# Eight-row pieces for two query weight chunks, and a cache copy cut into pieces of 15 rows down to 1

## The reference, cut to what matters

```python
# per layer
h = x + merge(A(xn), B(xn), C(xn)) @ w_out        # xn = rms(x)
# PEER, xb = rms(h): 256 prompt tokens and 32 sample tokens
q = (xb @ wq).reshape(blk, 8, 2, 128)             # 8 heads, two half queries
s1 = einsum('nhd,kd->nhk', q[:, :, 0], k1)
s2 = einsum('nhd,kd->nhk', q[:, :, 1], k2)
...                                               # top 16 of each, top 16 of the sums: e, g
hid = gelu(einsum('nd,nhkd->nhk', xb, eu[e]))
y = h + einsum('nhk,nhkd->nd', g * hid, ev[e])
# the sample group's caches move on by four rows
kvs2048[l] = concat([cache_a_kv_w2048[l], new rows])[-2048:]
```

## Time and profile before

| | us |
|---|---|
| median of 3 runs | 1813.08 |
| lowest and highest of them | 1811.39, 1815.6 |
| the profiled execution, its own time | 1812.33 |
| its span in the trace | 1810.3 |

### The profile page before, as it was taken

One profiled execution on the slowest core, in us unless ns is written; L12 is line 12 of the kernel. 1 busy time (PEld: TensorE's weight loads), 2 busy tenths in 40 slices (PEclk: granted clock), 3 DMA queues, 4 the chain that ended last, 5 costly groups with the idle time before them and its releaser, 6 DMA issues.

```text
span 1810.3 us, 18420 instructions
## 1 busy us (share of the span) xinstructions
PE 1546.9 (85%) x5782; PEld 826.0 (46%) x5782; DVE 1109.4 (61%) x2783; ACT 605.1 (33%) x1873; POOL 696.6 (38%) x682
## 2 busy tenths in 40 slices
PE   8999999998888787788789999989888877877777
PEld 5779644454333232233257885545443333322221
DVE  3545765676888774444535367475878878644444
ACT  2332432333334332222333344233333323322222
POOL 5211443455444443334313014435455444433341
PEclk9999999999889989999799999999999989899999
DMA  9899999999999999999979999999999999999996
GB/s 337 343 377 378 382 422 421 413 421 421 421 421 421 422 421 422 422 422 421 422 282 399 380 387 371 421 421 418 421 421 421 422 421 421 422 422 421 422 423 288
DMA packets 102839, 730.03 MB, mean 403 GB/s; under 512 B 14994, under 2 KB 16115, under 8 KB 21973
## 3 DMA queue, kind: packets, MB, share of 16 engines
q0 software_dynamic: 90432, 627.75, 84.2%
q1 hardware_dynamic: 11760, 100.48, 14.0%
q10 hardware_dynamic: 548, 0.62, 0.1%
HBM read 724.54 MB, written 48.10 MB: 427 GB/s over the span
## 4 chain that ended last, share of the span: by engine, by line
DMA 45%; PE 37%; DVE 11%; ACT 3%; issue 2%; DVEq 2%; ACTq 1%; POOL 0%; POOLq 0%
DMA arena<-peer_uv,idx 26%; PE bank L1767 19%; DMA wring<-peer_uv,idx 10%; PE bank L1522 7%; DMA yt<-peer_uv,idx 3%; PE bank L1690 3%; DVE arena L1344 3%; DMA qf<-peer_uv,idx 3%; DVE wring L1344 2%; DMA wring<-w_out 2%; PE bank L1731 2%; PE bank L1517 1%; ACT diag L867 1%; DVE yt L1344 1%; DVE route L1316 1%
## 5 line engine op out<-in xcount | busy, mean ns | idle before, releaser
L1767 PE MATMUL bank<-arena,diag 128*128 128x512 f32 (+1 forms) x1416 | 669.3, 616 | 114.0 <-ACT diag L867 114.0
L1344 DVE SCALAR_TENSOR_TENSOR arena<-arena,xn 128x1024 f32<-128x1024 f32 x378 | 457.9, 1224 | 329.1 <-DMA arena<-peer_uv,idx 327.9
L642 POOL DMA_INDIRECT arena<-peer_uv,idx x378 | 407.2, 1077 | 594.0 <-PE bank L1767 439.4
L1767 PEld LDWEIGHTS bank<-arena,diag 128*128 128x128 f32 (+1 forms) x1416 | 261.8, 191 | 477.5 <-issue 295.2
L859 ACT ACTIVATE act<-hid 128x2 f32<-128x2 f32 x287 | 58.4, 204 | 907.5 <-DVE arena L1344 600.5
L1767 PE MATMUL bank<-wring,diag 128*128 128x512 f32 x336 | 170.8, 649 | 47.8 <-ACT diag L867 47.8
L867 ACT ACTIVATE diag<-ident,weight 128x128 f32<-128x128 f32 (+1 forms) x574 | 194.3, 385 | 20.9 <-issue 1.4
L642 POOL DMA_INDIRECT wring<-peer_uv,idx x84 | 96.6, 1150 | 144.8 <-PE bank L1767 137.4
L862 ACT ACTIVATE weight<-act,gate 128x1 f32<-128x1 f32 x574 | 138.0, 287 | 19.8
L1344 DVE SCALAR_TENSOR_TENSOR wring<-wring,xn 128x1024 f32<-128x1024 f32 x84 | 102.2, 1225 | 66.1 <-DMA wring<-peer_uv,idx 64.8
L1767 PE MATMUL bank<-qf,diag 128*128 128x512 f32 (+1 forms) x216 | 108.0, 637 | 39.7 <-ACT diag L867 39.7
(11 more groups left out here) (290 smaller groups left out, 1571.3 us busy)
## 6 DMA issues: line engine op xcount, KB each, us to landing
kvs<-cache_a_kv_w SPq DMA_DIRECT2D x32, 1022.0 KB, 10.7
wring<-w_col SPq DMA_DIRECT2D x15, 1024.0 KB, 8.5
wring<-w_tok SPq DMA_DIRECT2D x8, 1408.0 KB, 8.7
arena<-peer_wq SPq DMA_DIRECT2D x10, 1024.0 KB, 14.9
kvs<-cache_a_kv_w SPq DMA_DIRECT2D x16, 508.0 KB, 12.5
arena<-peer_uv,idx POOLq DMA_INDIRECT x378, 20.6
qf<-cache_keys POOLq DMA_DIRECT2D x8, 576.0 KB, 11.2
qf<-cache_values POOLq DMA_DIRECT2D x8, 576.0 KB, 21.6
```

Of the source, the lines that this page charges most:

```text
L642: pool.indirect_dma_start(out=ring[j], out_offset=None, in_=io["peer_uv"], in_offset=bass.IndirectOffsetOnAxis(ap=idx[:, n:n + 1], axis=0) ...
L1344: last = v.scalar_tensor_tensor(out=ring[j][:, 0:D], in0=ring[j][:, 0:D], scalar=1.0, in1=xn[:, i, :], op0=ALU.mult, op1=ALU.mult, accum_o ...
L1767: last = pe.matmul(bank[b0 + half][0:r, :], diag[:, n % 16, 0:r], ring[SLOT_OF[n]][:, D + 512 * half:D + 512 * half + 512], start=False, s ...
```

## The change

Three things. Chunks 6 and 7 of the query weights, in both layers, are loaded by `load_q_rows`: sixteen transfers of eight partitions each (8 rows of 8 KB, 64 KB) in the place of one of 128. All sixteen count on the same semaphore, and PE waits for 16 times as much. The first cache copy of layer 1 is made by `shift_shares`: the same bytes in nine transfers. Eight of them have 15, 13, 11, 9, 7, 5, 3 and 1 rows of 4079 floats (16.3 KB a row, 64 rows together), and a last one has the 576 floats that are left, as 16 rows of 36. The final wait counts eight transfers more.

```diff
+WQ_PIECES = 16
+SHARES = (15, 13, 11, 9, 7, 5, 3, 1)
+SHARE = 4079
...
+            def load_q_rows(l, chunk):
+
+                for r in range(0, P, P // WQ_PIECES):
+                    sp.dma_start(wq_home(chunk)[r:r + P // WQ_PIECES], io["peer_wq"][l, chunk, r:r + P // WQ_PIECES]).then_inc(wq_loaded[chunk], 16)
...
+            def shift_shares(l, b):
+
+                d_ = io["kvs2048"].rearrange("l b r k h d -> l b (r k h d)")[l, b, 0:(2048 - NT) * 128]
+                s_ = io["cache_a_kv_w2048"].rearrange("l b r k h d -> l b (r k h d)")[l, b, NT * 256:NT * 256 + (2048 - NT) * 128]
+                at_ = 0
+                for k in SHARES:
+                    sp.dma_start(d_[at_:at_ + SHARE * k].rearrange("(q n) -> q n", q=k),
+                                 s_[at_:at_ + SHARE * k].rearrange("(q n) -> q n", q=k)).then_inc(shift_out, 16)
+                    at_ += SHARE * k
+                sp.dma_start(d_[at_:].rearrange("(q n) -> q n", q=16), s_[at_:].rearrange("(q n) -> q n", q=16)).then_inc(shift_out, 16)
...
-                        shift(l, m)
+                        if l and m == 0:
+                            shift_shares(l, 0)
+                        else:
+                            shift(l, m)
...
                 sp.wait_ge(qf_ps, NQ * l + q_count(4, 1, WHOLE))
-                load_q(l, 6)
+                load_q_rows(l, 6)
                 sp.wait_ge(qf_ps, NQ * l + q_count(1, 1, REST))
-                load_q(l, 7)
+                load_q_rows(l, 7)
...
-            sp.wait_ge(shift_out, 16 * 4 * NB * DEPTH)
+            sp.wait_ge(shift_out, 16 * (4 * NB * DEPTH + len(SHARES)))
...
-                pe.wait_ge(wq_loaded[chunk], 16 * (l + 1))
+                pe.wait_ge(wq_loaded[chunk], 16 * (WQ_PIECES if chunk > 5 else 1) * (l + 1))
```

## The result

The changed kernel takes 1870.19 us (median of 5 runs, 1869.18 to 1877.0), the kernel before 1812.19 (5 runs). The ratio is 1.0319, with a 95% interval from 1.0305 to 1.0333: 58 us slower, far outside the range of the prediction. The profiled execution took 1869.18 us, with a span of 1867.3, so 57.0 us more than before's 1810.3.

A forecast was written before the change was run, and what follows sets the result against it. Bound by the DMA engines, exactly the last of sixteen. Layer 0 gives +2.6 - 1.9 = +0.7, layer 1 +2.6: +3.3 on 1812.33, so 1815.6 us, range 1808.5 to 1823.5.

The forecast's parts named there:

- What bounds the kernel: In the gather stretches: the DMA engines at 421 GB/s, exactly the last of sixteen, since dots wait for the last part.
- late engine: One DMA engine ending layer 0's gathers 8.1 us behind the mean, layer 1's 7.2; forecast placed it in the upper eight.
- the price of the chunks: Chunks 6 and 7, both layers: 0 if engines rotate, 2.49 us per chunk if always the same eight; completions up to 0.8.
- The load itself: Behind the chunk loads: eight engines get +4.98 us a layer, the others -4.98; each layer ends 2.6 us later.
- rival A: Late engine among the loaded eight: 2 x 4.98 plus 1.24 of copy, 11.2 us, so 1823.5; chance 0.20.
- my hint for the upper half: The instruction-fetch queue with 8 KB packets is the highest-numbered; 53 such packets on one engine would make it late.
- a lead of the late engine: Behind chunk 7: 4.98 us less work for the late engine, lost because relieved engines run dry until gathers come.
- rival B: The relieved late engine keeps its 4.98 us; loaded eight end last, -2.2 and -1.4, so 1808.7; chance 0.15.
- The copy: Layer 1's first cache copy, in layer 0's tail: pieces relieve the late engine by 1.9 us, between 0 and 2.49.
- What hides the chunks' own landing: Chunk 6 lands by 277.8, wanted at 305.15; chunk 7 by 322.1, wanted at 341.79, 19.7 us to spare.
- Rival C: Small transfers rotate or rows are cut further, all engines get the same: chunks 0, copy 0, 1812.8; chance 0.13.
- The sign in GB/s: Behind chunk 7, fewer than 378 and 394 GB/s: half the engines still for 5 us is 130 less over 8 us.

The follow-up runs named there:

- the copy's kernel: Only the cache copy cut into the change's pieces, chunks 6 and 7 as single transfers, against the kernel before: 1812.91 us, ratio 0.9999.

## Why the prediction was wrong, point by point

- **What bounds the kernel: right.** The DMA engines' pace, one late engine, and a dot that waits for the last part: the experiments can be read by it, and what is lost at a chunk load is still missing at the end.
- **The failing step is the price of the chunks.** I bounded it between 0 and 2.49 us for each chunk (3.3 with the completions), as a matter of how many rows an engine gets, each row at 0.311 us, and never asked where a transfer's rows land at the same time. The rows of before that I went by could not show it, since the chunks and gathers there all cover 128 partitions; but a bound that reckons engines alone isn't a bound. A loss of 12 to 16 us for each chunk was outside both of its ends and of all rivals. The runs show 0.63 us in place of 0.311 for each 8 KB, of the gathers' rows too, while the pieces are under way. This is some 47 of the 58 us, when the load's 9.8 and the copy's 1.2 are taken off.
- **The load itself was right as a mechanism, and mis-sized.** With the collisions away, the eight engines' load costs 9.8 us (8.5 to 12.9), the cost of sixteen small transfers included. The forecast had 5.2 for the two layers, since it put the late engine in the other half; rival A, which had it in the loaded half, had 10.0. In the trace of that kernel the four stretches behind the chunk loads are longer than before by 2.7, 1.3, 2.0 and 1.6 us (7.6 together), by these rows of SP and its span of 1821.6:

```profile
256.01 17.51 SPq L475 DMA_DIRECT2D arena<-peer_wq  x16
307.85 17.77 SPq L475 DMA_DIRECT2D xn<-peer_wq  x16
...
733.05 0.82 SPq L463 DMA_DIRECT2D wring<-w_tok  x2
...
1150.45 17.00 SPq L475 DMA_DIRECT2D arena<-peer_wq  x16
1201.68 16.62 SPq L475 DMA_DIRECT2D xn<-peer_wq  x16
```

  Chunk 6 costs its full 2.49 or near it, chunk 7 less; that the engines ran dry there before may be why, and is not shown. What separates 7.6 in this one trace from 9.8 in the timed runs is open: 3 us of this trace's extra span lie ahead of chunk 6, and no run shows where they come from.
- **The late engine: rival A was right, the forecast wrong.** It sits among the loaded eight, as the fourth of them as far as the order of the pieces tells. So it is neither of the two engines, 7 and 15, that the prediction took from the Trainium skill ("DMA: Bandwidth & Descriptors", section "Latency and other measured facts") as the usual slow ones; the measurement decides. The queue's number, my hint for the upper half, was worth nothing. What would have become of a lead of the late engine, lost or kept (rival B), was therefore never put to the test.
- **The copy: right in its amounts, wrong in its sign.** I took -1.9 us. The late engine has six pieces for four, which is +1.24, rival A's figure. The changed kernel's own tail has it:

```profile
938.90 1.23 DVE L1366 SCALAR_TENSOR_TENSOR qf<-qf,xn 128x1024 f32<-128x1024 f32 x1 [1.26 <-DMA qf<-peer_uv,idx]
...
952.44 1.23 DVE L1366 SCALAR_TENSOR_TENSOR arena<-arena,xn 128x1024 f32<-128x1024 f32 x1 [1.24 <-DMA arena<-peer_uv,idx]
```

  13.54 us for 12.28. It is too small to be seen in the time of the copy's kernel, whose stretch has it too (13.52).
- **What hides the chunks' own landing: right, with the landing too short.** Chunk 7 was to land 20 us after its issue at the latest, and took 27 (345.5 - 318.17), for 10.4 before. The cover was long enough for that: even from the old issue, 301.90 + 27.3 = 329.2 is ahead of 341.79.
- **Rival C, that the transfers rotate or are cut further: wrong here.** The one kernel in which it came true is another: transfers contiguous on both sides were cut further, and so spread even in spite of their eight rows.
- **The sign in GB/s was the right place to look, for another reason.** The rate behind chunk 7 was to fall by 130 over 8 us because half the engines stood still. It fell by 188 to 221 over 20 us, already behind chunk 6, and with a share of 1.02, so not from engines that stood still.

## What to carry to other kernels

While other transfers keep the DMA engines busy, the price of a small load into SBUF depends on the set of partitions that it covers, and not only on its bytes and rows: don't cut a load into blocks of adjacent partitions. If pieces must be small, spread each over the partitions: on every fourth partition the loss was 24 us in place of 59, and 9.8 where all pieces went to the half in which no such meeting was seen. To cut along the free dimension, so that each piece still covers all 128 partitions, should avoid the matter, but no run here tried it. A badly placed load of 1 MB cost 12 to 16 us, though nobody waited for it, because it slowed the packets of the gathers; a DMA share of 1.0 with half the GB/s is the sign of it.

## What the runs showed of the hardware

- With eight rows a transfer on adjacent partitions, a busy DMA system fell from 421 to between 200 and 233 GB/s with its engines' share at 1.02 (1.01 before); 8 KB of a gather took 0.63 us for 0.31. With every fourth partition of the lower half it stayed at 420, with the upper half it fell to between 300 and 313.
- Transfers to sixteen adjacent partitions, on sixteen engines and with even shares, still cost 32.6 us for four chunks.
- One DMA engine (the fourth, if a transfer of k rows goes to the first k) is 4 to 5 us behind all others at the end of a layer. Work given to it delays the layer's last dot one to one: 1.24, 2.48 and 7.50 us for 2, 4 and 12 pieces of 0.62.
- A DRAM-to-DRAM transfer written as 8 rows of 65 KB went out in 16 equal data packets of 32.7 KB; rows of 4079 floats kept their shape.
